# Neighbourhood attention: the place of the next step's scores in TensorE's order

## The reference, cut to what matters

```
s_loc = jnp.einsum('bnqhd,bnkhd->bhnqk', qr, ks_) + bias
s_loc = jnp.where(mask, s_loc, NEG_INF)
s_ctx = jnp.einsum('bnqhd,bkhd->bhnqk', qr, kc)
p = jax.nn.softmax(jnp.concatenate([s_loc, s_ctx], axis=-1), axis=-1)
o = (jnp.einsum('bhnqk,bnkhd->bnqhd', p[..., :nk], vs_)
     + jnp.einsum('bhnqk,bkhd->bnqhd', p[..., nk:], vc))
```

## Time and profile before

| | |
|---|---|
| median of 3 runs | 3402.44 us (3401.86 to 3402.96) |
| the profiled execution, its time | 3402.71 us |
| its span | 3401.0 us |
| TensorE busy with matmuls | 3197.3 us, 94% of the span |
| VectorE busy | 1669.3 us, 49% |
| ScalarE busy | 1212.6 us, 36% |
| GpSimd busy | 747.6 us, 22% |
| mean granted clock of TensorE | 0.976 |

### The profile page before, as it was taken

The page is one execution under the profiler, slowest core; times in us unless marked ns, Lnnn a source line. Parts: engine busy times, 40 slices in busy tenths (PEclk is TensorE's granted clock), DMA queues, the critical chain, the costliest instruction groups (busy, mean ns, idle before and its releaser), DMA issues.

```text
span 3401.0 us, 39869 instructions
## 1 busy us (share of the span) xinstructions
PE 3197.3 (94%) x16156; PEld 2513.5 (74%) x16156; DVE 1669.3 (49%) x2507; ACT 1212.6 (36%) x2068; POOL 747.6 (22%) x578
## 2 busy tenths in 40 slices
PE   6989988899988999989899999999999999999998
PEld 4777667677767788867788778887888776578886
DVE  2256564425664534456655553446444525564344
ACT  3242265433274322233344332234222325542222
POOL 2234302333504000056332300001000343230000
PEclk9999999999999999999899999999999999999999
DMA  5213200221102222222000133232232231022322
GB/s 226 93 37 129 99 24 28 74 69 54 58 20 79 89 93 100 88 93 90 16 8 1 56 100 104 93 99 83 89 105 87 77 111 38 1 89 92 109 86 79
DMA packets 77575, 260.55 MB, mean 77 GB/s; under 512 B 8400, under 2 KB 9552, under 8 KB 76240
## 3 DMA queue, kind: packets, MB, share of 16 engines
q1 hardware_dynamic: 76528, 253.28, 22.4%
q0 software_dynamic: 864, 4.72, 0.4%
HBM read 255.87 MB, written 2.10 MB: 76 GB/s over the span
## 4 chain that ended last, share of the span: by engine, by line
PE 85%; DVE 7%; ACT 4%; issue 2%; POOL 1%; DMA 1%; SPq 0%; ACTq 0%; DVEq 0%; POOLq 0%
PE banks L345 83%; PE banks L354 2%; DVE area L576 1%; DVE x_lat L579 1%; POOL w_lo L336 1%; DMA area<-in_w_mod 1%; DVE small L1797 0%; DVE area L1741 0%; DVE area L538 0%; DVE area L1779 0%; ACT area L434 0%; POOL w_late L336 0%; ACT area L437 0%; ACT w_hi L326 0%; DVE area L494 0%
## 5 line engine op out<-in xcount | busy, mean ns | idle before, releaser
L345 PE MATMUL banks<-area,w_hi 128*128 128x512 f32 (+4 forms) x5896 | 1770.5, 383 | 22.6 <-ACT area L532 7.4
L345 PEld LDWEIGHTS banks<-area,w_hi 128*128 128x128 f32 (+2 forms) x5896 | 1078.7, 188 | 288.4 <-issue 22.6
L345 PE MATMUL banks<-area,w_lo 128*128 128x512 f32 (+4 forms) x2948 | 1120.6, 381 | 0.0
L345 PEld LDWEIGHTS banks<-area,w_lo 128*128 128x128 f32 (+2 forms) x2948 | 555.0, 188 | 119.0
L345 PE MATMUL banks<-area,w_late 128*128 128x512 f32 (+2 forms) x2316 | 580.4, 399 | 28.8 <-ACT area L532 14.8
L326 ACT ACTIVATE w_hi<-w_raw 128x1024 fp32r<-128x1024 f32 (+2 forms) x361 | 349.5, 971 | 547.0 <-PE banks L345 419.5
L345 PEld LDWEIGHTS banks<-area,w_late 128*128 128x128 f32 (+1 forms) x2316 | 435.5, 191 | 146.7 <-ACT area L532 18.1
L345 PE MATMUL banks<-area,area 64*128 64x256 f32 (+11 forms) x3464 | 423.1, 338 | 59.4 <-DMA area<-in_w_mod 15.6
L410 POOL TENSOR_TENSOR area<-area,area 128x512 f32<-128x512 f32 (+1 forms) x102 | 139.5, 1370 | 1477.2 <-ACT area L395 1475.5
L345 PEld LDWEIGHTS banks<-area,area 128*128 128x128 f32 (+4 forms) x3464 | 337.4, 184 | 135.1 <-issue 55.1
L336 POOL TENSOR_TENSOR w_lo<-w_raw,w_hi 128x1024 fp32r<-128x1024 f32 (+1 forms) x133 | 305.1, 2296 | 397.4 <-ACT w_hi L326 397.4
(11 more groups left out here) (236 smaller groups left out, 2307.8 us busy)
## 6 DMA issues: line engine op xcount, KB each, us to landing
w_raw<-in_l_ffn_w_in SPq DMA_DIRECT2D x176, 512.0 KB, 3.2
w_raw<-in_l_ffn_w_out SPq DMA_DIRECT2D x128, 384.0 KB, 3.0
w_raw<-in_w_in SPq DMA_DIRECT2D x66, 512.0 KB, 3.5
w_raw<-in_w_mod SPq DMA_DIRECT2D x32, 512.0 KB, 4.6
w_raw<-in_w_qkv SPq DMA_DIRECT2D x24, 512.0 KB, 3.3
w_raw<-in_l_w_in SPq DMA_DIRECT2D x22, 512.0 KB, 3.2
w_raw<-in_w_out SPq DMA_DIRECT2D x32, 320.0 KB, 2.9
area<-in_w_mod SPq DMA_DIRECT2D x8, 1024.0 KB, 16.6
```

The costliest lines, as they stand in the source:

```text
L345: return e.matmul(out, lhsT, rhs, start=first, stop=stop, skip_group_check=True)
```

## The change

The three calls in TensorE's loop change places. The scores of k+1 come first, then the values of k-3 and the transposes of k-2. What each of them issues and waits for is the same as before, and so are the programs of all other engines.

```diff
                 self.scores_pe(q, e, 0)
                 for k in range(self.n + 3):
+                    if k + 1 < self.n:
+                        self.scores_pe(q, e, k + 1)
                     if k >= 3:
                         self.values_pe(q, e, k - 3)
                     if 2 <= k < self.n + 2:
                         self.turn_pe(q, e, k - 2)
-                    if k + 1 < self.n:
-                        self.scores_pe(q, e, k + 1)
```

## The result

The changed kernel takes 3459.8 us (median of 4 runs, 3454.3 to 3468.2) against 3402.5 us (median of 4 runs). The ratio is 1.0171, with a 95% interval of 1.0153 to 1.0188: 57 us slower. The profiled execution is the quickest of the four, 3454.3 us with a span of 3452.6.

What follows compares the result with a forecast made beforehand. TensorE, holding 85% of the chain, was taken as the bound. Longer steps at full clock (+35.5 us) and half-clock stretches (21.6 us) gave +57 us on 3402.7, so 3460 us, range 3436 to 3490.

Steps and rivals of the forecast that it cites:

- The mechanism: TensorE: scores(k+2) wait for exponentials(k), which stand behind ScalarE's copy of transposes(k-2), with nothing left between; +35.5 us at full clock.
- A plain step: Scores to scores over values, half the transposes, ScalarE's copy and exponentials: 5.52 us, TensorE idle 2.2 us of it.
- A step with block 3: Step whose values end block 3, with VectorE's out_dve and two scalings in the chain: 6.84 us.
- The stages: Two neighbourhood stages at full clock: layer 0 87.0 us against 65.81, layer 1 68.5 against 54.23.
- 0.8 x 1.5: Half-clock term: 18 gaps, a share of 0.8 followed by a half-clock stretch, 1.5 us each; 21.6 us.
- What is queued behind the wait: Behind TensorE's wait: values(k-2), turn(k-1), then ScalarE's next copy, VectorE's out_dve and copy, GpSimd's identities; layer 1's tail 17.6 us.
- What I said would show it: Profile after: about 20 waits for line 1301, clock 0.7 to 0.85, stages 87 to 105 and 68 to 85 us.
- The clock rule: Skill's loop with one wait per pass, every pass restarting at half clock: share 1, 27 us, time 3465.
- A: Rival: same mechanism in the stages with the clock kept, +35.5, 3438 us; chance 0.15.
- B: Rival: clock stays at half through most of the stages, up to +89, 3491 us; chance 0.18.
- C: Rival: faster, gaps ahead of the values go if ScalarE's exponentials are done in time, 8.7 us, 3394 us; chance 0.03.
- D: Rival: no change, TensorE not held by the waiting scores or the wait off the path, 3403; chance 0.02.

Runs made afterwards that it cites:

- VectorE's edit: The kernel before, with VectorE taking the maxima of k and the sums of k-1 before out_dve of k-3: 3390.8 us, ratio 0.9963.
- The half move: The kernel before, with TensorE's order values, scores, transposes: 3420.6 us, ratio 1.0051.
- the first experiment: The changed kernel, with ScalarE taking the exponentials of k before its copy of the transposes of k-2: 3423.2 us, ratio 1.0061.
- the filled gaps: The changed kernel, with 12 small matmuls adding zeros behind the transposes in 6 passes of each stage: 3452.7 us, ratio 1.0145.

## Why the prediction was right

**The mechanism** is shown. The chain of a plain step is the forecast's, piece by piece, and undoing its one premise, that the copy stands ahead of the exponentials, took back nearly two thirds. Most of the rest is `out_dve`, which the forecast has in its steps of 6.84 and 6.51 us: with that moved too, the kernel with the early scores is 6 us faster than the kernel before, though 6 us slower than that one with VectorE's edit. The half move doesn't bear on this, since another wait of the same length came with it.

**A plain step** at the full clock: 5.52 forecast, 5.54 measured (220.71 to 226.25). **A step with block 3**: 6.84 forecast; at the full clock 6.85 in the first experiment (181.32 to 188.17), where `out_dve` stands in the same chain.

**The stages.** At the full clock I had 87.0 + 68.5 = 155.5 us. Measured are 178.5, so 23 us are left for the clock, where the forecast had 21.6. The 17 steps between the scores of 4 and the last took 70.2 and 49.8 us, 20 more than the 99.8 of the sum: 1.2 us a gap, as 0.8 x 1.5. In detail, 13 of the 17 steps ran partly at half clock and lost some 1.55 us each. The terms hold only as an average: single plain steps took 5.5 or between 6.8 and 8.0 us. Nor does a longer gap cost more in each case: behind 2.97 and 2.98 us (200.04 and 234.19) the step took 1.6 us more than its sum, behind 3.33 us (818.60) 2.5 us, and behind 2.92 us (208.14) nothing. The forecast's count had a slip: before there are six gaps of 2.18 to 2.28 us, not five. The sixth is this one of the kernel before, and behind it too TensorE ran at half clock (2.08 us for scores that take 1.13 at full), so the share was five of six:

```profile
752.77 2.08 PE L345 MATMUL banks<-area,area 64*128 64x256 f32 x8 [2.28 <-ACT area L1301]
```

That would have made the term 22.5 us in place of 21.6.

**What is queued behind the wait.** As told. In layer 1's tail the profile puts a wait of 2.50 us down to GpSimd's scaled identities. But those of this step had been made at 834.58, and VectorE's copy ended at 847.74, 0.10 us ahead of the values:

```profile
834.58 1.19 POOL L1373 TENSOR_SCALAR area<-const,small 128x128 f32<-128x128 f32 x2 [5.65 <-DVE small L1360]
...
847.07 0.67 DVE L1287 COPY area<-banks 128x512 f32<-128x512 f32 x1
...
847.84 0.44 PE L345 MATMUL banks<-area,const 128*64 128x128 f32 x4 [2.50 <-POOL area L1373]
```

The identities that GpSimd makes at 847.25 are the next step's. So the chain is the forecast's, over VectorE's copy: from the first maximum (844.95) to the values are 2.89 us, as forecast. The tail took 19.9 us (840.32 to 860.17) in place of 17.6, and the 2.3 us are half clock: 0.87 in the values ahead of `out_dve` (2.24 us from 841.38 to 843.62, for 1.37) and 1.40 in the step from 847.84 (4.57 us for 3.17).

**What I said would show it.** 22 waits for line 1301 against "about 20"; clocks of 0.84 and 0.79 in "0.7 to 0.85"; stages of 97.7 and 80.8 us in their ranges. Wrong was that all other stretches would be as long as before: in the profiled execution they were 6.8 us shorter. The same stretch varies by 6 us among the nine profiled executions, and the four times of the changed kernel by 14, so these runs show no cause in the change. That the median met the forecast within 1 us is luck in part: the stages' 58.4 us, against the 57.1 of the sum, are the better check, though they are those of one execution, the quickest of four.

**The clock rule.** A half-clock stretch in every pass would have given 3465 us. At the full clock throughout went 4 of the 17 steps in this execution (from 186.56, 208.14, 220.71 and 797.65). The Trainium skill's rule (TensorE: Matmul & The Clock Gate, HAM oscillation), told of a loop with longer waits than these, holds here in 13 passes of 17.

**The rivals.** A, with the clock kept, is out: the filled gaps gave back 9.0 us of the stages by the clock alone. B is out: the clocks are 0.79 and 0.84, and its 89 us weren't lost. C needed the exponentials ahead of the copy, which rows of ScalarE show they aren't. D is out by the 22 waits.

## What to carry to other kernels

In a pipeline written out by hand, the distance between a producer and the consumer that comes back to the same engine is cover. Before moving a call forward, list what stands between it and the call that its wait hangs on, through every queue on the way: here scores(k+2) hung on transposes(k-2) over ScalarE's queue, though no line of `scores_pe` names them. List as well what the moved call covered where it stood: in the half move the values lost the scores as cover, and TensorE stood 0.83 us for a copy. And look at which queue makes TensorE wait now: the two lines in VectorE's loop were worth 12 us, and no order tried with the early scores came below that.

## What the runs showed of the hardware

More work on TensorE made the kernel quicker: 24 small instructions of 1.61 us in a gap that they don't outlast kept the granted clock at 1.00 from 181.35 to 196 us, over gaps behind which it had fallen in most steps without them, and 12 passes with them gave back 9.0 us of the two stages.

The length of a gap alone doesn't tell whether the clock falls. In layer 0 of the changed kernel it fell behind waits of 2.97 and 2.98 us and stayed full behind one of 2.92 us (208.14); it fell in 7 of 10 steps there, and in 9 of 10 when `out_dve` stood late and the waits were 2.0 to 2.1 us.

In the profile a wait for several semaphores can be put down to the wrong engine: the 2.50 us at 847.84 bear GpSimd's name, whose work had been done 12 us earlier.
